# Fused two-block layer stack on one core: four score products in a row per attention step, the compressed block's turn first, squares and norms moved into the last step

## What is computed

```python
def block_fn(args):                      # 128 queries at a time, 8 heads, 2 key/value heads, head size 64
    s_c = jnp.einsum("bgrtd,bgnd->bgrtn", qb, k_cmp) * scale          # compressed keys (31 of them)
    p_c = masked_softmax(s_c, cmp_end[None, :] <= t[:, None])
    o_c = jnp.einsum("bgrtn,bgnd->bgrtd", p_c, v_cmp)
    ...
    s_s = jnp.einsum("bgrtd,bgtmd->bgrtm", qb, gk) * scale            # selected keys (all of them here)
    o_s = jnp.einsum("bgrtm,bgtmd->bgrtd", masked_softmax(s_s, mask_s), gv)
    ...
    s_w = jnp.einsum("bgrtd,bgkd->bgrtk", qb, kw) * scale             # window keys
    o_w = jnp.einsum("bgrtk,bgkd->bgrtd", masked_softmax(s_w, mask_w), vw)
    return o_c, o_s, o_w
o = gates[..., 0:1] * o_c + gates[..., 1:2] * o_s + gates[..., 2:3] * o_w
...
y = jnp.concatenate([rms_norm(y_nsa, g_nsa), rms_norm(y_gmlp, g_gmlp), rms_norm(y_conv, g_conv)], axis=-1)
x = x + y @ w_out[l]
```

## Time and profile before

| | |
|---|---|
| median of 3 runs | 2503.73 us (2503.28 to 2506.99) |
| profiled execution: span | 2501.5 us |
| around the span, if that execution was like the median | 2.2 us (2503.73 - 2501.5) |
| PE busy | 2483.6 us, 99% of the span |
| chain that ended last | PE 96%, DVE 3%, ACT 1% |
| second attention, scores of step 1 to turns of step 15 | 1835.8 to 1963.7 us |

### The profile page before, as it was taken

How to read it: one execution, slowest core, us unless ns; L and a number is a source line. 1 busy time by engine, 2 the same in 40 slices (tenths; PEclk the granted TensorE clock), 3 DMA queues, 4 the chain that set the end, 5 groups by cost and what they waited for, 6 DMA issues and landing times.

```text
span 2501.5 us, 34757 instructions
## 1 busy us (share of the span) xinstructions
PE 2483.6 (99%) x11914; PEld 2048.2 (82%) x11914; DVE 1228.8 (49%) x1436; ACT 915.9 (37%) x1324; POOL 1257.2 (50%) x878
## 2 busy tenths in 40 slices
PE   9999999999999999999999999999999999999998
PEld 8888888888888888888888888888877788888887
DVE  7444612453322542555135423227998755788364
ACT  5223433332222331334233322224367644444333
POOL 5555355555545545544455555545532443555454
PEclk9999999999999999999999999999999999999999
DMA  5332233333333333322333333337321232333332
GB/s 162 105 92 85 68 101 93 101 93 97 97 94 100 96 98 93 93 77 79 96 99 94 96 98 98 96 95 162 85 67 65 75 89 68 93 101 92 101 91 78
DMA packets 441982, 235.38 MB, mean 94 GB/s; under 512 B 16145, under 2 KB 436113, under 8 KB 441873
## 3 DMA queue, kind: packets, MB, share of 16 engines
q1 hardware_dynamic: 441440, 233.26, 32.5%
q10 hardware_dynamic: 432, 0.67, 0.1%
HBM read 231.81 MB, written 2.10 MB: 94 GB/s over the span
## 4 chain that ended last, share of the span: by engine, by line
PE 96%; DVE 3%; ACT 1%; issue 0%; DVEq 0%; POOL 0%; ACTq 0%; POOLq 0%
PE unit_ps L1848 62%; PE unit_ps L1993 13%; PE unit_ps L1979 7%; PE aux L1885 2%; PE o_banks L1885 1%; PE unit_ps L1885 1%; PE aux L2116 1%; PE unit_ps L2084 1%; PE aux L2222 1%; PE unit_ps L2157 1%; PE o_banks L1926 1%; DVE c_f L1314 1%; PE aux L2266 1%; PE aux L2054 0%; PE unit_ps L2090 0%; PE o_banks L2143 0%
## 5 line engine op out<-in xcount | busy, mean ns | idle before, releaser
L472 POOL TENSOR_TENSOR wl<-raw,wh 128x512 fp32r<-128x512 f32 x862 | 1250.9, 1472 | 1224.2 <-ACT wh L543 821.1
L543 ACT ACTIVATE wh<-raw 128x1024 fp32r<-128x1024 f32 x304 | 322.6, 1061 | 1023.9 <-PE unit_ps L1848 965.9
L1848 PE MATMUL unit_ps<-ah,wh 128*128 128x512 f32 x1280 | 502.5, 393 | 0.0
L1848 PE MATMUL unit_ps<-ah,wl 128*128 128x512 f32 x1280 | 498.1, 389 | 0.0
L1848 PE MATMUL unit_ps<-al,wh 128*128 128x512 f32 x1280 | 498.1, 389 | 0.0
L1848 PE MATMUL unit_ps<-bh,wh 128*128 128x512 f32 x768 | 299.7, 390 | 0.0
L1848 PE MATMUL unit_ps<-bl,wh 128*128 128x512 f32 x768 | 298.8, 389 | 0.0
L1848 PE MATMUL unit_ps<-bh,wl 128*128 128x512 f32 x768 | 298.8, 389 | 0.0
L1848 PEld LDWEIGHTS unit_ps<-ah,wh 128*128 128x128 f32 x1280 | 240.3, 188 | 51.3 <-issue 1.9
L1848 PEld LDWEIGHTS unit_ps<-al,wh 128*128 128x128 f32 x1280 | 240.3, 188 | 51.2 <-issue 1.9
L1848 PEld LDWEIGHTS unit_ps<-ah,wl 128*128 128x128 f32 x1280 | 240.2, 188 | 50.1
(11 more groups left out here) (404 smaller groups left out, 3864.3 us busy)
## 6 DMA issues: line engine op xcount, KB each, us to landing
raw<-w_in_dram SPq DMA_DIRECT2D x144, 512.0 KB, 4.0
raw<-w_up_dram SPq DMA_DIRECT2D x64, 512.0 KB, 4.0
raw<-w_down_dram SPq DMA_DIRECT2D x64, 512.0 KB, 4.1
raw<-up_dram SPq DMA_DIRECT2D x44, 512.0 KB, 3.8
raw<-w_conv_out_dram SPq DMA_DIRECT2D x16, 512.0 KB, 4.1
raw<-w_ret_out_dram SPq DMA_DIRECT2D x16, 512.0 KB, 4.1
raw<-w_o_dram SPq DMA_DIRECT2D x16, 512.0 KB, 4.1
raw<-down_dram SPq DMA_DIRECT2D x16, 512.0 KB, 3.9
```

The costliest lines, as they stand in the source:

```text
L472: last = pool.tensor_tensor(wl[j][:, half], raw[j % 2][:, half], wh[j][:, half].bitcast(F32), ALU.subtract)
L543: act.activation(wh[j][:], raw[j % 2][:], ACT.Copy).then_inc(w_hi, 1)
L1848: last = pe.matmul(unit_ps[j % 2][:], w[j][:, k], v[:, k * T:(k + 1) * T], start=(k == 0 and n == 0), stop=(k == KB - 1 and n == 2))
```

## The change

There are four edits. (1) `att_scores(k)` issues all four heads' scores and then four masks, where it issued two scores, two masks, two scores, two masks; and it now waits for all four exponentials of the step before, where the first pair waited for two. (2) In steps with b = 1 the compressed block is turned, copied and multiplied first, and the last key block ends the sum (`o_att`). (3) ACT's squares over the early tokens stand in turn 15 between the second copy and its half of `weigh(15)`, where they stood at the end of turn 14. (4) DVE's `first_norm(6)` and `first_norm(7)` stand in turn 15 after `weigh(15)`, where they stood in turn 14 ahead of `take_out(6)` and `weigh(15)`.

```diff
@@ -103,13 +103,13 @@
 STEPS2 = [(it, b, c, rp) for it, (c, rp) in enumerate(ITS) for b in range(2)]
 N_STEPS = len(STEPS2)
 
-TURNS = [(k, n) for k, (it, b, c, rp) in enumerate(STEPS2) for n in [*range(c + 1)] + [-1] * b]
+TURNS = [(k, n) for k, (it, b, c, rp) in enumerate(STEPS2) for n in [-1] * b + [*range(c + 1)]]
 KEY_TURNS = [turn for turn in TURNS if turn[1] >= 0]
 
 GM_STEP, CV_STEP = 4, 5
 TAPS_AT = [0, 0, 5, 6]
 GM_PARTS, CV_PARTS = 12, 13
-FIRST_NORMS = {8: (0, 1, 2, 3), 11: (4,), 12: (5,), 14: (6, 7)}
+FIRST_NORMS = {8: (0, 1, 2, 3), 11: (4,), 12: (5,), 15: (6, 7)}
 
 PART_ORDER = [4, 5, 6, 7, 0, 1, 2, 3]
 TINY = 1e-30
@@ -798,6 +798,9 @@
                     if more:
                         exp_head(k + 1, n)
                     if n == 1:
+                        if k == N_STEPS - 1:
+                            act.wait_ge(o_taken, len(ITS) - 2)
+                            nsa_squares(EARLY)
                         weigh(k)
                 for turn in turns[REP:]:
                     take_turn(*turn)
@@ -810,9 +813,6 @@
                     for n in range(2):
                         part_hi((0 if k == GM_PARTS else 2) + n)
                 mixer_norms(k)
-                if k == N_STEPS - 2:
-                    act.wait_ge(o_taken, len(ITS) - 2)
-                    nsa_squares(EARLY)
             for turn in turns_of(N_STEPS - 1):
                 take_turn(*turn)
             nsa_root(EARLY, 3)
@@ -2109,13 +2109,14 @@
                 lanes = slice(g * HD, g * HD + HD)
                 return lanes, q_t[r][lanes, c * P:(c + 1) * P]
 
-            def att_scores(k, i):
+            def att_scores(k):
                 it, b, c, rp = STEPS2[k]
-                for g in range(2):
-                    lanes, q = query(c, 2 * rp + i, g)
-                    pe.matmul(aux[:, 2 * i + g, 0:(c + 1) * P], q, k_att[b][lanes, 0:(c + 1) * P], start=True, stop=False)
-                for g in range(2):
-                    pe.matmul(aux[:, 2 * i + g, c * P:(c + 1) * P], diag_b[:, 0], diag_b[:, 1], start=False, stop=True).then_inc(s_att, 1)
+                for i in range(2):
+                    for g in range(2):
+                        lanes, q = query(c, 2 * rp + i, g)
+                        pe.matmul(aux[:, 2 * i + g, 0:(c + 1) * P], q, k_att[b][lanes, 0:(c + 1) * P], start=True, stop=False)
+                for h in range(REP):
+                    pe.matmul(aux[:, h, c * P:(c + 1) * P], diag_b[:, 0], diag_b[:, 1], start=False, stop=True).then_inc(s_att, 1)
 
             def compressed_scores():
                 for m in range(NC * REP):
@@ -2150,12 +2151,14 @@
                 pe.wait_ge(pt_ready, j + 1)
                 if n < 0:
                     for i in range(2):
-                        pe.matmul(unit_ps[1][:, i * P:(i + 1) * P], v_cmp[:, i], tmp[it % 2][:, 0:P], start=False, stop=(i == 1)).then_inc(o_att, 1)
+                        pe.matmul(unit_ps[1][:, i * P:(i + 1) * P], v_cmp[:, i], tmp[it % 2][:, 0:P], start=False, stop=False)
                 else:
                     for g in range(2):
                         lanes, cols = slice(g * HD, g * HD + HD), slice(2 * g * P, (2 * g + 2) * P)
-                        pe.matmul(unit_ps[1][lanes, 0:2 * P], v_att[b][:, n, lanes], pt_att[KEY_TURNS.index((k, n)) % 4][:, cols],
-                                  start=(b == 0 and n == 0), stop=False)
+                        last = pe.matmul(unit_ps[1][lanes, 0:2 * P], v_att[b][:, n, lanes], pt_att[KEY_TURNS.index((k, n)) % 4][:, cols],
+                                         start=(b == 0 and n == 0), stop=(b == 1 and n == c))
+                        if b == 1 and n == c:
+                            last.then_inc(o_att, 1)
 
             def turns_of(k):
                 return [j for j, turn in enumerate(TURNS) if turn[0] == k]
@@ -2190,15 +2193,13 @@
                             last.then_inc(mix_mm, 1)
             pe.wait_ge(evac, U2 + Z_Q + 4)
             pe.wait_ge(mem_lo, KB)
-            for i in range(2):
-                att_scores(0, i)
+            att_scores(0)
             z(Z_Q + 3)
             for k in range(N_STEPS):
 
                 if k + 1 < N_STEPS:
-                    for i in range(2):
-                        pe.wait_ge(exp_att, REP * k + 2 * i + 2)
-                        att_scores(k + 1, i)
+                    pe.wait_ge(exp_att, REP * (k + 1))
+                    att_scores(k + 1)
                 mixer_mean(k)
                 if k == 0:
                     pe.wait_ge(evac, U2 + NZ + 2)
```

## The result

The changed kernel takes 2512.72 us (median of 6 runs, 2510.02 to 2515.33) beside 2504.01 us for the kernel before (6 runs, 2503.28 to 2506.99). The ratio is 1.0033, with a 95% interval of 1.0024 to 1.0043. It is slower by about 8 us, where I had forecast no measurable difference and 2507.2 us as the upper end.

What follows compares the result with a forecast made beforehand. PE was taken as the bound, busy 2483.6 of 2501.5 us. Work -5.3, waits removed at the end -1.7 and waits added +7.7 gave +0.7 us, 2504.4 us likeliest, range 2499.8 to 2507.2.

Steps and rivals of the forecast that it cites:

- Edit 1 on PE: Score steps of the second attention: fewer changes between scores and masks save 0.28 us a step, 4.5 us in sixteen.
- edit 2's 0.8 us on PE: Eight steps with b = 1: one change between full and half width fewer, 0.1 us each, 0.8 in all.
- the rival by the Trainium skill's rule: Second pair's first weight load in each group of four isn't covered: 1.7 us at most, 2506.1 us, chance 0.06.
- The late first mask: First maxima can start two score passes later, 0.85 to 0.21 us by width; DVE and ACT follow late, PE waits.
- The signs named for the maxima and for L1281: Changed profile: 384-column maxima start 1.8 us behind scores; PE idles 0.5 us or more for L1281 in turns 4, 5, 6.
- turn 5, whose slack was to absorb 0.36 us: In turn 5 the copy began 0.45 us after the maxima, so some 0.36 of the 0.64 us delay is absorbed.
- only the first term grows, by 0.64: Turn 4, chain from scores through maxima and copy to PE's next product: only the maxima's start moves, PE +0.64 us.
- 7.7 added less 1.7 removed: PE's waits over the whole change: 7.7 us added, 1.7 us removed at the end.
- That cover is 0.1 us thick: Early mean: DVE's norms and sums end at 1967.6, PE arrives at 1967.7; if gone, only what is missing is lost.
- Little waits are added: Behind turn 6, idle time of DVE and ACT takes up their delay: -2.3 us, 2501.4 us, chance 0.30.
- the whole gain: No wait is added anywhere: -5.3 - 1.7 = -7.0 us, 2496.7 us, chance 0.07.
- DVE becomes the bound: DVE's idle time ahead of maxima is shorter than two passes in every step: +7.1 us, 2510.8 us, chance 0.04.

Runs made afterwards that it cites:

- only_turns: The kernel before with edit 2 alone, the compressed block first: 2505.69 us beside 2505.57, ratio 1.0003.
- before_thin: The kernel before with GpSimd's subtractions for weights streaming during the attention cut to 8 columns: 2502.65 us beside 2505.16 for the kernel before.
- after_thin: The changed kernel with GpSimd's subtractions for weights streaming during the attention cut to 8 columns: 2503.19 us beside 2505.01 for the kernel before, ratio 0.9990.
- only_end: The kernel before with edits 3 and 4 alone, squares and two first norms in turn 15: 2505.59 us beside 2505.57, ratio 1.0006.
- only_scores: The kernel before with edit 1 alone, four scores, then four masks, one wait for all four exponentials: 2514.53 us beside 2505.57, ratio 1.0045.
- mean_first_scores_thin: Edit 1 alone, with the mean ahead of scores on PE, its reading ahead of maxima on DVE, GpSimd's subtractions cut: 2504.63 us beside 2505.01, ratio 0.9993.

## Why the prediction was wrong

- **Edit 1 on PE: right.** A step saves 0.30 us on PE, where 0.28 was forecast. Sixteen of them are 4.8, and PE's busy time fell by 4.9 us for all edits together, so edit 2's 0.8 us on PE are hardly seen there. By itself edit 2 does save work: PE is busy 2481.6 us in `only_turns`, 2.0 less than before, but its waits are 4.5 us instead of 2.7. The loads of the second pair start 0.54 and 0.97 us behind the first scores of step 2, under scores that run for 1.99 us; the rival by the Trainium skill's rule falls.
- **The late first mask: right in kind, place and, up to turn 4, size.** Against the kernel before, less the 1.15 us at entry, PE is +0.36 at scores 2 (+0.4 forecast) and +0.05 at scores 5 (0). The signs named for the maxima and for L1281 in turns 4, 5 and 6 are there, and so are those for L726 ahead of scores 2 and 13 (0.64 and 0.58 us); the one ahead of scores 9 is 0.26, under the 0.5 named. In the pair of thin kernels PE loses 2.3 us from scores 5 to scores 8, where +2.0 was forecast. The 0.3 more is turn 5, whose slack was to absorb 0.36 us and absorbed none: both pairs lose 0.6 there.
- **The step that failed: "only the first term grows, by 0.64", in turn 4, and each later step built on it.** The sum took DVE's instructions at the durations they had before. After turn 4 PE is at +1.83, not +0.87; at scores 8 +3.26, not +2.0; at scores 9 +3.30, not +1.9; at scores 13 +6.05, not +2.7; at turn 15 +4.56, not +0.7; at the early mean +6.6, not +0.7. The largest differences are DVE instructions met by GpSimd's: L1314 in turn 4, L1539 ahead of the maxima of step 9, L1493 in turn 10, and the sums at the end. The net of the waits was mis-sized: 11.1 us measured, where 7.7 added less 1.7 removed is 6.0. That the omission was this one is shown by `before_thin` and `after_thin`: without GpSimd's work the net of the waits is 5.8 us, and the difference of the times 0.5 where the prediction had +0.7. That these come so close to the forecast is partly luck: the 1.7 us of waits to be removed are not in `before_thin`, and PE loses less than forecast ahead of scores 5.
- **"That cover is 0.1 us thick": right, and too lightly taken.** I noted that the norms now stand ahead of the sums, and priced the sums by an undisturbed row, and the norms by one that GpSimd had lengthened (2.46 us for 1.54). Even without edit 1 the wait was 1.9 us (`only_end`). The wait for `weigh(15)` was to be for ACT; it is 0.56 us and for DVE's half.
- **Two small slips.** Scores 9 at 1912.8 instead of 1910.99 are +1.8 and not +1.9. And an execution takes 1.8 us more than its span (2510.83 and 2509.1), not 2.2. Neither changes the outcome.
- **Rivals.** "Little waits are added" and "the whole gain" fall. "DVE becomes the bound" gave 2510.8 us and came nearest, but not by its mechanism: DVE still stood 1.75 us idle ahead of the maxima in turn 6. The number was close by accident. The chance of 0.04 was too small for what the profile showed of a stage in which DVE was busy 109.5 of 128.4 us, with a third engine whose rows I had not laid beside DVE's.

What is left open: the profiled spans differ by 7.6 us. Waits and saved work account for some 6.2 of them and the late entry for 1.15. In both executions the clock is full as long as PE works, so this is no effect of the clock. The medians differ by 8.7; the 1.1 us more goes with falls of the clock in other executions, whose cause isn't settled.

## What to carry to other kernels

Before an instruction of a busy engine is moved by a few tenths of a microsecond, lay the timeline of any engine that lengthens its instructions somewhere in the trace (here GpSimd for DVE) beside the new place, and price each instruction on the critical link at its slow duration (here 1.77 us for 0.69) as the upper bound. Ask the same of a wait that is to be removed: both waits of the end were there only through such a lengthened instruction. Grouping operations saves their change-over once, but delays the first result by all that now stands ahead of it: 4.9 us saved, 5.8 us waited, before any collision. When a wait is removed, read what stands next in the queue of the engine that releases the following wait; here the norms went from one side of a wait to the other side of the next, and reordering two calls gave back 2.7 us.

## What the runs showed of the hardware

DVE's instructions with two inputs in SBUF are held up by GpSimd's subtraction: 1.77 us instead of 0.69 for an addition that starts 0.04 us behind GpSimd. So is one with a tensor and a column of scalars in SBUF (L1539, 1.97 us instead of 1.13 for two). Those that read PSUM aren't: the maxima take 2.02 us with or without GpSimd beside them. Over the whole execution DVE is busy 1228.8 us in the kernel before and 1213.2 in `before_thin`, 1230.3 in the changed one and 1213.7 in `after_thin`. So the GpSimd work that was cut (that of 24 weight units) lengthens DVE's by 15.6 and 16.6 us; the change hardly adds collisions, it moves them to where PE waits. By the Trainium skill (SBUF — State Buffer, "Who interferes with whom") a DVE instruction with two SBUF inputs contends with a GpSimd instruction that reads SBUF, the port pair that they share is an exclusive lock, and the order of issue decides who blocks. The trace agrees: the lengthened addition of turn 10 starts just behind GpSimd's subtraction, and gains 1.08 us, less than the 1.25 us that one of the pair takes.

The granted clock differs between executions of one kernel. The kernel before has 2502.77 to 2504.34 us at a mean granted clock of 0.999, and 2509.74 to 2510.47 at 0.996. The six executions of the changed kernel lie at 0.996 to 0.998, those at 0.998 at 2510.02 and 2510.83 us. Equal means are not equal clocks here. Behind PE's last product the clock is at its lower level, and this tail is longer in the changed kernel. The profiled executions, first of the kernel before, then of the changed one; the columns are those of the earlier trace rows, the granted clock the third from the end:

```profile
2495.50:2501.50 6.00, 0.00 (x0) 0.00 (x0) 2.77 (x7) 0.00 (x0) 0.00 (x0) 0.50 0.78 262
```

```profile
2500.30:2509.00 8.70, 0.00 (x0) 0.00 (x0) 5.16 (x9) 0.16 (x1) 1.81 (x3) 0.51 0.71 241
```

Ahead of these tails the clock is full in both, and their means are 0.999 and 0.998. So some 7.6 of the 8.7 us is there at an equal clock. In the profiled execution of `only_scores` the clock fell to the lower level (1.2 GHz) in two places:

```profile
1838.00:1841.00 3.00, 3.00 (x56) 2.98 (x54) 2.83 (x4) 0.00 (x0) 1.25 (x2) 1.00 0.14 29
1841.00:1845.00 4.00, 4.00 (x30) 3.94 (x28) 3.63 (x6) 3.58 (x9) 0.00 (x0) 0.57 0.38 113
1968.00:1971.10 3.10, 1.45 (x10) 1.00 (x11) 2.55 (x8) 1.70 (x6) 1.45 (x1) 1.00 0.12 23
1971.10:1974.50 3.40, 3.40 (x9) 2.63 (x8) 0.90 (x2) 2.52 (x4) 2.71 (x2) 0.50 0.49 138
```

Ahead of the first fall PE had been busy for 3 us without a gap; just ahead of the second it had stood still for 1.65 of 3.1 us. A mean of 0.57 over 4 us and of 0.50 over 3.4 us takes away 1.7 us of full clock each time. Kernels with more waits tend to a lower mean clock (0.996 on average for `only_scores`, 0.998 for `before_thin`), but `mean_first_scores_thin` had 0.997 with 5.8 us of waits, fewer than the 6.8 of `after_thin`, which had 0.998. I did not isolate what lowers it.
